# First normalisation by tiles of x, first weights in two pieces: a hybrid attention and mixture-of-experts layer on one core

## The reference, cut to what matters

```
xn = x * rsqrt(mean(x*x, -1) + 1e-5) * ln1_w
proj = xn @ w_in                      # 1024 x 9744: attention q/k/v, GLA q/k/v/gate, gate code, merge gates
o_a, o_b = dilated attention(proj), gated linear attention(proj)
h = x + (sigmoid(g_a)*(o_a @ w_proj_a) + sigmoid(g_b)*(o_b @ w_proj_b)) @ w_out
h = h + MoE(rms_norm(h))              # top 4 of 32 experts, w_up 1024 x 2048, w_down 1024 x 1024 each
out = rms_norm(h)
```

## Time and profile before

| | us |
|---|---|
| median of 3 runs | 1238.17 |
| lowest and highest | 1237.89, 1239.25 |
| the profiled execution | 1238.62 |
| its span, first to last instruction | 1236.9 |

### The profile page before, as it was taken

One profiled execution on the slowest core, in us unless ns is written; L12 is line 12 of the kernel. 1 busy time (PEld: TensorE's weight loads), 2 busy tenths in 40 slices (PEclk: granted clock), 3 DMA queues, 4 the chain that ended last, 5 costly groups with the idle time before them and its releaser, 6 DMA issues.

```text
span 1236.9 us, 16260 instructions
## 1 busy us (share of the span) xinstructions
PE 1160.7 (94%) x6982; PEld 593.0 (48%) x6983; DVE 392.3 (32%) x673; ACT 241.5 (20%) x334; POOL 10.8 (1%) x29
## 2 busy tenths in 40 slices
PE   9999999999999999998988989898989898989997
PEld 8888888888633343333333333333333333333332
DVE  7766646756531122211111111121211111111112
ACT  5344446544410000100000000000100010000002
POOL 2000000000000000000000000000000000000000
PEclk9999999999999999999999999999999999999999
DMA  8745333496999999999999999999999999999996
GB/s 267 257 170 182 137 136 136 154 393 227 375 431 424 434 430 430 432 429 434 428 436 429 433 430 433 431 431 432 431 432 431 432 429 436 428 437 428 425 423 281
DMA packets 47725, 456.95 MB, mean 369 GB/s; under 512 B 5732, under 2 KB 5880, under 8 KB 31784
## 3 DMA queue, kind: packets, MB, share of 16 engines
q1 hardware_dynamic: 47384, 455.62, 88.4%
q10 hardware_dynamic: 304, 0.79, 0.2%
HBM read 455.35 MB, written 1.05 MB: 369 GB/s over the span
## 4 chain that ended last, share of the span: by engine, by line
PE 59%; DMA 38%; DVE 1%; SPq 1%; issue 0%; ACT 0%; DVEq 0%
PE ps L1453 57%; DMA ring<-in_w_up_dram 30%; DMA arena<-in_w_up_dram 5%; DMA ring<-in_w_down_dram 2%; DMA ring<-in_w_in_dram 1%; PE ps L1976 1%; SPq L565 0%; DVE w_split L937 0%; PE ps L1648 0%; PE ps L1860 0%; DVE arena L982 0%; PE ps L1758 0%; ACT w_split L650 0%; DVE arena L983 0%; DVE bias_p L981 0%
## 5 line engine op out<-in xcount | busy, mean ns | idle before, releaser
L1453 PE MATMUL ps<-ring,arena 128*64 128x512 f32 x2304 | 524.5, 608 | 48.7 <-DMA ring<-in_w_up_dram 47.1
L1453 PEld LDWEIGHTS ps<-ring,arena 128*64 128x64 f32 x2304 | 163.6, 140 | 379.2 <-issue 299.5
L1453 PE MATMUL ps<-arena 128*64 128x512 f32 (+3 forms) x920 | 200.9, 558 | 18.5 <-DMA arena<-in_w_up_dram 18.5
L1372 DVE TENSOR_SCALAR arena<-ps 128x512 f32<-128x512 f32 x32 | 22.1, 692 | 484.8 <-PE ps L1453 484.8
L1453 PEld LDWEIGHTS ps<-arena 128*64 128x64 f32 (+1 forms) x920 | 77.7, 148 | 128.7 <-issue 98.1
L937 DVE TENSOR_TENSOR w_split<-ring,w_split 128x2048 fp32r<-128x2048 f32 x48 | 109.8, 2291 | 75.3 <-ACT w_split L650 75.3
L843 ACT ACTIVATE arena<-arena 128x512 f32<-128x512 f32 x32 | 20.2, 632 | 549.7 <-DVE arena L1372 549.7
L1453 PE MATMUL ps<-w_split,x_split 128*128 128x512 f32 x528 | 123.2, 392 | 0.1
L650 ACT ACTIVATE w_split<-ring 128x2048 fp32r<-128x2048 f32 x47 | 89.7, 1915 | 104.2 <-PE ps L1453 93.5
L1453 PEld LDWEIGHTS ps<-w_split,x_split 128*128 128x128 f32 x528 | 98.4, 188 | 20.7 <-issue 0.3
L1453 PE MATMUL ps<-x_split,w_split 128*128 128x256 f32 (+1 forms) x544 | 93.1, 331 | 0.1
(11 more groups left out here) (248 smaller groups left out, 603.4 us busy)
## 6 DMA issues: line engine op xcount, KB each, us to landing
ring<-in_w_up_dram SPq DMA_DIRECT2D x38, 4096.0 KB, 31.1
ring<-in_w_down_dram SPq DMA_DIRECT2D x19, 4096.0 KB, 29.9
arena<-in_w_up_dram SPq DMA_DIRECT2D x12, 4096.0 KB, 30.5
ring<-in_w_in_dram SPq DMA_DIRECT2D x17, 2048.0 KB, 7.7
ring<-in_w_up_dram SPq DMA_DIRECT2D x16, 2048.0 KB, 11.4
arena<-in_w_down_dram SPq DMA_DIRECT2D x7, 4096.0 KB, 30.4
arena<-in_w_up_dram SPq DMA_DIRECT2D x7, 2048.0 KB, 14.8
ring<-in_w_down_dram SPq DMA_DIRECT2D x6, 2048.0 KB, 18.4
```

Of the source, the lines that this page charges most:

```text
L1372: dve.tensor_scalar(glu_c, ps[bank][:, :], LIMIT, None, ALU.min).then_inc(glu_ok, 1)
L1453: return pe.matmul(dst, lhsT, rhs, start=start, stop=stop, skip_group_check=True)
```

## The change

SP and ScalarE's queue each load 64 partitions (`CAP` = 64) of both tiles, tile 0 first, so a tile has landed when its semaphore is at 32. The squares of each tile are divided by columns: VectorE has 512 of tile 0 and 384 of tile 1, and its sum starts from EPS and is scaled by 1/D; ScalarE has the rest. VectorE's sum goes into ScalarE's root as its bias. Reciprocal, diagonal and normed products then follow tile by tile, and VectorE's squares of tile 1 stand behind the diagonal of tile 0. TensorE's fills are 40 before the transpose of ln1_w and 4 between the tiles, in place of 46 and 16. The first half of chunk 0 is loaded in two DMAs of two k tiles (the second counts on `lnf_in`, whose later wait goes to 32), ScalarE copies each when it is there, and the first products take all four output tiles for k 0 and 1, then for k 2 and 3.

```diff
+        SQ_COLS = (512, 384)
+
         @block.sync
         def _(sp):
-            sp.dma_start(h_sb[:, 0, :], x[0, 0:P, :]).then_inc(x_in[0], 16)
+            for t in range(TT):
+                sp.dma_start(h_sb[0:CAP, t, :], x[0, t * P:t * P + CAP, :]).then_inc(x_in[t], 16)
...
-                    sp.dma_start(dst[:, 0:4, :], dense_src(c)[:, 0:4, :]).then_inc(part_in[c], 16)
+                    if c == 0:
+                        sp.dma_start(dst[:, 0:2, :], dense_src(c)[:, 0:2, :]).then_inc(part_in[c], 16)
+                        sp.dma_start(dst[:, 2:4, :], dense_src(c)[:, 2:4, :]).then_inc(lnf_in, 16)
+                    else:
+                        sp.dma_start(dst[:, 0:4, :], dense_src(c)[:, 0:4, :]).then_inc(part_in[c], 16)
...
         @block.scalar
         def _(act):
-            act.dma_start(h_sb[:, 1, :], x[0, P:SEQ, :]).then_inc(x_in[1], 16)
+            for t in range(TT):
+                act.dma_start(h_sb[CAP:P, t, :], x[0, t * P + CAP:t * P + P, :]).then_inc(x_in[t], 16)
             act.dma_start(ln1_r, ln1_w[0].rearrange("(k p) -> k p", p=P)).then_inc(ln1_in, 16)
 
             act.wait_ge(early_ok, 2)
             act.activation(warm[:, 0:1], epsc[:, 0:1], ACT.Sqrt)
-            act.wait_ge(x_in[1], 16)
-            act.activation(xs[:, 1, :], h_sb[:, 1, :], ACT.Square, accum_out=ssq[:, 1:2]).then_inc(sq1_ok, 1)
-            act.wait_ge(ssq_ok, 1)
-            act.activation(rstd[:, 0:1], ssq[:, 0:1], ACT.Sqrt, bias=epsc[:, 0:1], scale=1.0 / D).then_inc(root_ok, 1)
-            act.wait_ge(sq1_ok, 1)
-            act.activation(rstd[:, 1:2], ssq[:, 1:2], ACT.Sqrt, bias=epsc[:, 0:1], scale=1.0 / D).then_inc(root_ok, 1)
+            for t in range(TT):
+                act.wait_ge(x_in[t], 32)
+                act.activation(xs[:, t, SQ_COLS[t]:D], h_sb[:, t, SQ_COLS[t]:D], ACT.Square,
+                               accum_out=ssq[:, t:t + 1]).then_inc(sq1_ok, 1)
+                act.wait_ge(sq1_ok, t + 1)
+                act.wait_ge(ssq_ok, t + 1)
+                act.activation(rstd[:, t:t + 1], ssq[:, t:t + 1], ACT.Sqrt, bias=ssq4[:, t, 0:1], scale=1.0 / D)\
+                   .then_inc(root_ok, 1)
...
-            act.activation(split_w(0, 0)[:, :, 0:SEQ], half_chunk(0)[:, :, 0:SEQ], ACT.Copy).then_inc(w_part_ok, 1)
-            act.activation(split_w(0, 0)[:, :, SEQ:512], half_chunk(0)[:, :, SEQ:512], ACT.Copy).then_inc(w_high_ok, 1)
-            act.wait_ge(rstd_ok, 1)
+            act.activation(split_w(0, 0)[:, 0:2, :], half_chunk(0)[:, 0:2, :], ACT.Copy).then_inc(w_part_ok, 1)
+            act.wait_ge(lnf_in, 16)
+            act.activation(split_w(0, 0)[:, 2:4, :], half_chunk(0)[:, 2:4, :], ACT.Copy).then_inc(w_high_ok, 1)
+            act.wait_ge(rstd_ok, 2)
...
-            dve.wait_ge(x_in[0], 16)
-            dve.tensor_tensor_reduce(xs[:, 0, :], h_sb[:, 0, :], h_sb[:, 0, :], 1.0, 0.0, ALU.mult, ALU.add,
-                                     ssq[:, 0:1]).then_inc(ssq_ok, 1)
+            def x_inverse(t):
+                dve.wait_ge(root_ok, t + 1)
+                dve.reciprocal(rstd[:, t:t + 1], rstd[:, t:t + 1]).then_inc(rstd_ok, 1)
+                dve.wait_ge(rstd_ok, t + 1)
+                dve.tensor_scalar(diag[:, t, :], ident[:, :], rstd[:, t:t + 1], None, ALU.mult).then_inc(diag_ok, 1)
+
+            def x_squares(t):
+                dve.wait_ge(x_in[t], 32)
+                dve.tensor_tensor_reduce(xs[:, t, 0:SQ_COLS[t]], h_sb[:, t, 0:SQ_COLS[t]], h_sb[:, t, 0:SQ_COLS[t]],
+                                         1.0 / D, EPS, ALU.mult, ALU.add, ssq4[:, t, 0:1]).then_inc(ssq_ok, 1)
+
+            x_squares(0)
+            dve.wait_ge(ident_ok, 2)
+            x_inverse(0)
+            x_squares(1)
             dve.wait_ge(ln1_ps, 1)
             dve.tensor_copy(ln1T, ps[6][:, 0:KT])
-            dve.wait_ge(root_ok, 2)
-            dve.reciprocal(rstd[:, :], rstd[:, :]).then_inc(rstd_ok, 1)
-            dve.wait_ge(rstd_ok, 1)
-            dve.wait_ge(ident_ok, 2)
-            for t in range(TT):
-                dve.tensor_scalar(diag[:, t, :], ident[:, :], rstd[:, t:t + 1], None, ALU.mult).then_inc(diag_ok, 1)
+            x_inverse(1)
...
-            fill(46)
+            fill(40)
             pe.wait_ge(ident_ok, 2)
             pe.wait_ge(ln1_in, 16)
             pe.transpose(ps[6][:, 0:KT], ln1_r, ident[0:KT, 0:KT]).then_inc(ln1_ps, 1)
-            fill(16)
-
-            def normed_x(b):
-
-                for t in range(TT):
-                    if b == 0:
-                        pe.wait_ge(diag_ok, t + 1)
+
+            def normed_x(t):
+
+                pe.wait_ge(diag_ok, t + 1)
+                for b in range(2):
                     for n in range(2):
                         k = 2 * b + n
                         ins = mm(ps[2 + b][:, n * SEQ + t * P:n * SEQ + t * P + P], h_sb[:, t, k * P:k * P + P],
                                  diag[:, t, :], t + n == 0, True)
-                ins.then_inc(xT_ps, 1)
+                    if t:
+                        ins.then_inc(xT_ps, 1)
 
             normed_x(0)
+            fill(4)
             normed_x(1)
...
-                pe.wait_ge(w_part_ok, 1)
-                for half in range(2):
+                for half, w_ready in enumerate((w_part_ok, w_high_ok)):
+                    pe.wait_ge(w_ready, 1)
                     pe.wait_ge(x_high_ok, half + 1)
-                    first_products(0, 0, 0, (0, 1), True, False, range(2 * half, 2 * half + 2))
-                pe.wait_ge(w_high_ok, 1)
-                first_products(0, 0, 0, (2, 3), True, False)
+                    first_products(0, 0, 0, range(4), True, False, range(2 * half, 2 * half + 2))
```

More of the change, by code:

```diff
@@ L1434, in last_inverse @@
                 dve.wait_ge(last_rstd, t + 1)
-            dve.wait_ge(lnf_in, 16)
+            dve.wait_ge(lnf_in, 32)
             for q in (2, 3):
```

## The result

The kernel after takes **1241.03 us** (median of 10 runs, 1240.37 to 1242.85), the kernel before 1238.17 (10 runs, 1237.70 to 1239.25): a ratio of 1.0025, interval 1.0016 to 1.0033. The forecast was 1237.1, range 1235.9 to 1239.6; the change makes the kernel slower by 2.9 us, and the prediction was wrong in sign and outside its range. The prediction had called 2.5 us what a measurement can tell, and gave 0.04 to a slower kernel beyond that. The profiled execution took 1240.88 with a span of 1239.2, 2.3 more than before on both.

A forecast was written before the change was run, and what follows sets the result against it. TensorE and DMA share the bound; only the first 35 us change, by the smaller gain of TensorE's path and chunk 1's landing. 1.1 us off the median 1238.17 gave 1237.1, range 1235.9 to 1239.6.

The forecast's parts named there:

- With both queues on tile 0 first, its 0.52 MB are there at 3.8 … I take 4.4. Tile 1 as now, 5.8: Loads of x at the start: tile 0 lands at 4.4 us, tile 1 unchanged at 5.8.
- rival 2: x's halves don't arrive in tile order, tile 0 lands at 5.6 as now: 0.2 us won, 1238.0; chance 0.07.
- The transpose of ln1 stays at 6.15 (it waits for a load).: TensorE ahead of x's products: ln1's transpose keeps its start at 6.15 us, since it waits for a load.
- The issues that this adds … hidden: Added DMA issues at the start, one per queue and one for chunk 0: under 0.6 us each, hidden behind transfers.
- The 18 fills that go are worth nothing, they stood in idle time.: TensorE's dummy matmuls around normed x: removing 18 neither gains nor costs time; their cover was left to rival 4.
- rival 4: TensorE's clock falls in its gaps with 18 fewer fills, a fall put at 1.6 us: 1238.7; chance 0.05.
- Forecast 33.45: Start of unit 4's products on TensorE after the dense stage's unit 3: 33.45 to 33.5 us, against 34.61 before.
- The costs of the steps: TensorE's path from x to first products: tile 0's products 6.4, scaled transposes 11.3, gain 1.1 us.
- the dense and expert stages follow one to one: Time saved before the dense stage's products shifts everything behind, one for one; later stages get no shorter.
- The landing's path: Weight chunk 1's second half, landed at 19.39, gates unit 4 through the splits; full gain needs landing by 18.3.
- my estimate that it shrinks with what is left: Chunk 1's lag: instruction packet moves from 14.5 to 15.7, with 0.7 us of transfer left; landing 16.8 to 17.9.
- Rival 3: Slower: instruction packet comes sooner, at 13.5, chunk 1's second half lands at 21.0: 1239.8 us; chance 0.12.

The follow-up runs named there:

- e15: The changed kernel with its partition halves, ln1 loaded first on ScalarE's queue and long 512-column fills in all of TensorE's gaps: 1239.82 us, ratio 1.0010.
- e13: The changed kernel with x split by columns between the queues and fills in the gaps, mostly long 512-column ones: 1238.03 us, ratio 0.9996.
- e1: The changed kernel with x loaded as before, one whole tile on each queue: 1238.62 us, ratio 1.0002.
- e4: The changed kernel with each tile of x split by columns between the two queues, all 128 partitions each: 1237.92 us, ratio 0.9996.
- e7: The changed kernel with both tiles of x loaded whole on SP's queue, tile 0 first: 1238.29 us, ratio 0.9998.
- e2: The kernel before with nothing but x's loads by halves of the partitions on both queues: 1242.22 us, ratio 1.0037.
- e5: The changed kernel, loads untouched, with 76 fills instead of 40 ahead of ln1's transpose: 1240.47 us, ratio 1.0017.
- e9: The kernel before with 40 and 4 fills in place of 46 and 16, nothing else: 1238.66 us, ratio 1.0005.
- e11: The changed kernel with its partition halves, ln1 loaded first on ScalarE's queue and short fills (46, 16, 20) in TensorE's gaps: 1240.35 us, ratio 1.0016.
- e10: The changed kernel with x split by columns, 42 fills ahead of ln1's transpose and 10 behind tile 1's products: 1238.13 us, ratio 1.0001.
- e12: The kernel before with its fills as 11 long 512-column and 2 short ones, then 5 long: 1238.39 us, ratio 1.0000.
- e14: The changed kernel with both tiles whole on SP's queue in order and fills mostly as long 512-column ones: 1238.63 us, ratio 1.0000.
- e8: The changed kernel with x loaded as before in whole tiles, and fills back to 46 and 16 around ln1's transpose: 1238.14 us, ratio 0.9999.
- e16: e13 with fills of 13, 2 and 4 long, and ln1's transpose moved behind tile 0's products: 1238.25 us, ratio 0.9999.
- e6: The changed kernel with ln1 issued ahead of x on ScalarE's queue, fills unchanged: 1241.33 us, ratio 1.0022.
- e3: The changed kernel with SP loading the even partitions of each tile of x and ScalarE's queue the odd ones: 1240.53 us, ratio 1.0017.

## Why the prediction was wrong

**The step that failed first: "With both queues on tile 0 first, its 0.52 MB are there at 3.8 … I take 4.4. Tile 1 as now, 5.8".** I took the rate of the earlier trace rows for the halves too; those rows are transfers to all 128 partitions. Measured: 5.5 and 8.1. The rate depends on which partitions a transfer writes: halves 194 to 292 GB/s, even and odd rows 310 to 365, columns 342 to 399 but for one microsecond of 293. The price of it alone, against loads that land as forecast, is e15 against e13: 35.48 - 33.27 = 2.2 us of unit 4. In the medians the whole slowdown goes with the halves: e1, e4 and e7, without them, can't be told from the kernel before, and e2, with nothing but them, has all of it. The Trainium skill has the rule that I overlooked (SBUF — State Buffer, Door 1: The DMA port swizzle): partitions 0 to 63 reach only 8 of 16 ports and move 196 GB/s at 1 MiB, hardly more than 32 partitions do. The trace agrees in direction: with both halves in flight the rows show 194 to 292, nearer to that figure than to the 422 before; no run has one half alone. That the two halves in flight together don't add up is on the same page (section Can I just issue two DMAs to hit both halves?: one tile at partition 0 and one at 64 gave 6% more than a single one), and the trace agrees: 1.45 MB in the time of 2.17. Even and odd rows reach all ports by the formula of Door 1, and the rows show less than full rate for them, so the rule doesn't give the whole size there. The rule that I did cite (DMA: Bandwidth & Descriptors, Rules for kernel authors: halves serialize) I read as "nothing to gain"; here there was something to lose. I gave rival 2 tile 0's landing as late as 5.6, but no rival a later tile 1.

**"The transpose of ln1 stays at 6.15 (it waits for a load)."** The load is behind x on ScalarE's queue, and x became slower: 8.65. I had named the wait and not asked what would move it. TensorE runs in order, so tile 0's diagonal, ready at 7.2, waited too. "The issues that this adds … hidden" was off as well: two issues took 1.22 us on SP's queue and 1.47 on ScalarE's, against 0.85 and 0.89 for columns in e13, and ln1's own issue moved from 1.24 to 2.33.

**"The 18 fills that go are worth nothing, they stood in idle time."** The clock rose during them, at 6.56, and in the kernel after TensorE was out of fills at 5.58, ahead of any rise. There the idle time is 3.07 and the products of normed x take 4.1 instead of 2.05; e5 wins back 1.22 of the transposes' start with fills alone, and TensorE is through unit 3 at 36.17 instead of 37.38. e9's profile shows the same in the kernel before. This was rival 4, given 0.05 and 1.6 us, taken alone and as a fall in a gap of 0.54; what came was a rise that didn't happen, beside the gap that the loads made. Its 1.6 us was no measure either: in the kernel before that fall of the expert stage is a single stretch of 3.4 us at 0.50, from 535.6 to 539.0, behind five microseconds in which TensorE was busy for 2.81.

**The sum of the miss.** Forecast 33.45, measured 37.31: 3.9. e13 stands at 33.27, e15 at 35.48: halves 2.2. From e15 to the kernel after 1.8: 1.2 of clock (e5 through unit 3 at 36.17 against 37.38) and 0.6 for the rest, ln1's place in the queue above all (e5 against e15). These are differences of single profiles, good to some tenths. Against the kernel before, e15 is only 0.9 later at unit 4: what working by tiles and shared squares win is in that figure, set against the halves.

**What held.** The costs of the steps once loads and clock are right (e13, one execution). And that the dense and expert stages follow one to one: the span less unit 4's start is 1202.3 before, 1201.9 after, and 1201.6 to 1203.5 in all eighteen profiles. **The landing's path** held in its mechanism, with a term mis-sized. The pair of packet and landing of chunk 1's second half, in eight of the profiles (e5, e11 and after load x by halves):

| | before | e4 | e5 | e10 | e11 | e12 | e13 | after |
|---|---|---|---|---|---|---|---|---|
| packet at | 14.56 | 15.94 | 16.33 | 13.92 | 11.99 | 17.33 | 17.22 | 19.39 |
| landing | 19.39 | 18.99 | 21.32 | 19.47 | 21.79 | 17.15 | 17.11 | 18.89 |

Fills in other numbers move the packet, as they would if it is TensorE's code. With x at full rate a packet at 17 or later leaves a landing at 16.9 to 17.1 in e1, e9, e12, e13 and e14; one inside the transfer goes with a landing 1.4 to 2.6 us later (e7: packet 15.52, landing 18.50; e8: 14.89 and 19.73). With x by halves the landing is 18.89 behind the late packet of the kernel after, and 21.32 and 21.79 in e5 and e11, 2.4 and 2.9 more. So the lag before the change, which the prediction counted as 3.0 from 16.4, was 2.3 from 17.1. And my estimate that it shrinks with what is left (packet at 15.7, landing 16.8 to 17.9) was too good: e4 has 15.94 and 18.99. How much of that is the packet isn't settled, since e4 and e7 have late engines too, and e16 landed at 19.29 with its packet at 17.52. It decided nothing, since in the kernel after TensorE was 3 us late. Without fills the packet came at 19.39, not at the 15.7 that I had counted from: TensorE reached that instruction later.

Rival 3, my case for slower, named the packet; it was late, not early. The cause that came true had no case: a slower x, with rival 4's clock on top, would have been one.

## What to carry to other kernels

Split a load between two queues by columns, or give one queue both tiles in order, but not by halves of the partitions; read a rate from rows of transfers that write the same partitions as the new one. Before dummy products are called free, look at where in them the clock rises and at the length of the first real products behind them; and take few long ones rather than many short ones if instruction fetches fall into a transfer that others wait for. For each wait ahead of the work that a change moves, ask what stands in front of it on its queue.

## What the runs showed that I had not expected

- **The clock rises at different times behind the same work.** TensorE does the same in e4, e6 and the kernel after until its 40 fills end at 5.58. The clock's first record is at 5.59 in e4 and 5.81 in e6, which had ln1's transpose right behind the fills, and at 13.45 in the kernel after, which had nothing; e7, with the same 40 fills, has it at 4.53, while the fills still ran, and took 4.01 for them instead of 4.45. It falls again in gaps too: to 0.50 at 9.22 in e6, behind a wait of 1.47 and within one of 1.03, and at 9.43 in e2, behind one of 2.35. In e5 it held through 1.57. What decides when it rises or falls, no run settles. If executions of one kernel differ in the same way, that would explain part of the scatter (e13's runs go from 1236.81 to 1239.03); with one trace for each kernel this isn't shown.
- **Engines that fall behind.** In e4, e7 and e10 the rate at 5 us dips to 293, 266 and 307, with loads that write all 128 partitions. e13 has e10's loads and moves 393:

```profile
GB/s 0 20 276 402 381 307 375 387 395 391 408 397 395 397 373 426 180 84 45 88 274 395 403 410 403 246 130 13 14 90 94 240 403 401 414 395 205 0 33 203
```

```profile
GB/s 0 20 207 383 367 393 401 406 401 391 391 383 379 389 391 430 242 82 35 209 381 403 410 406 307 164 30 92 124 338 383 381 403 408 90 39 0 133 340 406
```

  The first is e10, the second e13. The cause stays open; it is no part of the slowdown, since e4 and e7 with it are as fast as the kernel before.
- **Even and odd rows don't restore the rate**, though each such load reaches from the first partitions to the last: 310 to 365 GB/s (e3). Not followed further.
